# The loop over two layers written out: one copy of the program per layer on each engine

## The reference

```python
def first_block(x, positions, ...):
    cos, sin = rope_tables(positions)
    h = x
    for l in range(DEPTH):          # DEPTH = 2, D_MODEL = 1024, D_FF = 2816
        h = layer_norm(DEEPNORM_ALPHA * h + 0.5 * swiglu(h, ffn1_w_gate[l], ffn1_w_up[l], ffn1_w_down[l]),
                       ln1_g[l], ln1_b[l])
        mix = hybrid_mixer(h, cos, sin, w_in[l], b_gate[l], ...)   # delta rule, convolution, attention
        h = layer_norm(DEEPNORM_ALPHA * h + mix, ln2_g[l], ln2_b[l])
        h = layer_norm(DEEPNORM_ALPHA * h + 0.5 * swiglu(h, ffn2_w_gate[l], ffn2_w_up[l], ffn2_w_down[l]),
                       ln3_g[l], ln3_b[l])
    return h

def swiglu(x, w_gate, w_up, w_down):
    return (jax.nn.silu(x @ w_gate) * (x @ w_up)) @ w_down
```

## Time and profile before

| what | value |
|---|---|
| time, median of 3 runs | 3097.96 us (3096.59 to 3101.69) |
| the profiled execution, its span | 3106.6 us |
| PE busy in it | 2952.7 us, 95% |
| DVE, ACT, POOL busy | 2016.3, 1454.0, 50.5 us |
| TensorE's mean granted clock | 0.968 of full speed |
| the first block's two layers | 0 to about 1628 us |

### The profile page before, as it was taken

How to read it: one execution, slowest core, us unless ns; L and a number is a source line. 1 busy time by engine, 2 the same in 40 slices (tenths; PEclk the granted TensorE clock), 3 DMA queues, 4 the chain that set the end, 5 groups by cost and what they waited for, 6 DMA issues and landing times.

```text
span 3106.6 us, 44687 instructions
## 1 busy us (share of the span) xinstructions
PE 2952.7 (95%) x16782; PEld 2488.4 (80%) x16782; DVE 2016.3 (65%) x2457; ACT 1454.0 (47%) x1612; POOL 50.5 (2%) x93
## 2 busy tenths in 40 slices
PE   7999898999899998899999999998999999999997
PEld 7998886599899988766997599554888888888886
DVE  6767862377677679325770355143887888888987
ACT  5443521144344453213431154233777667766765
POOL 2000010000000000000000000000000000000000
PEclk9999989999899999989999999998999999999999
DMA  8754412287576543117763365323999999999995
GB/s 288 243 168 162 156 55 70 95 271 237 181 266 229 184 134 106 46 59 239 244 216 108 123 194 171 116 101 108 329 341 329 352 333 342 327 350 339 337 331 215
DMA packets 396807, 659.84 MB, mean 212 GB/s; under 512 B 12010, under 2 KB 239192, under 8 KB 396696
## 3 DMA queue, kind: packets, MB, share of 16 engines
q1 hardware_dynamic: 396696, 658.32, 61.5%
HBM read 657.23 MB, written 1.05 MB: 212 GB/s over the span
## 4 chain that ended last, share of the span: by engine, by line
PE 71%; DVE 9%; PEld 6%; issue 5%; ACT 4%; DVEq 2%; DMA 1%; PEldq 1%; ACTq 1%; SPq 0%
PE banks L711 18%; PE banks L712 17%; PE banks L713 17%; PE banks L2085 3%; PE banks L2117 3%; PE banks L1389 2%; PE banks L707 1%; PE banks L879 1%; PE banks L784 1%; PEld banks L1225 1%; DVE expert_rest L1113 1%; DVE ffn_arena L1052 1%; DVE mod_sum L1045 1%; PEld banks L711 1%; PE banks L885 1%
## 5 line engine op out<-in xcount | busy, mean ns | idle before, releaser
L711 PE MATMUL banks<-ffn_arena 128*128 128x256 f32 (+1 forms) x3460 | 1164.6, 337 | 43.2 <-DVE ffn_arena L1073 17.2
L713 PE MATMUL banks<-ffn_arena 128*128 128x256 f32 (+1 forms) x3460 | 1149.7, 332 | 0.0
L711 PEld LDWEIGHTS banks<-ffn_arena 128*128 128x128 f32 x3460 | 661.6, 191 | 117.7 <-issue 39.1
L713 PEld LDWEIGHTS banks<-ffn_arena 128*128 128x128 f32 x3460 | 661.0, 191 | 68.8
L1113 DVE TENSOR_TENSOR expert_rest<-expert_raw,ffn_arena 128x2048 fp32r<-128x2048 f32 (+1 forms) x306 | 646.1, 2159 | 85.8 <-ACT ffn_arena L972 81.4
L712 PE MATMUL banks<-ffn_arena 128*128 128x256 f32 (+1 forms) x2200 | 672.9, 306 | 0.0
L972 ACT ACTIVATE ffn_arena<-expert_raw 128x2048 fp32r<-128x2048 f32 (+1 forms) x306 | 538.9, 1816 | 110.4 <-PE banks L713 107.2
L712 PE MATMUL banks<-expert_rest,ffn_arena 128*128 128x512 f32 (+1 forms) x1224 | 466.6, 381 | 0.0
L712 PEld LDWEIGHTS banks<-ffn_arena 128*128 128x128 f32 x2200 | 423.9, 193 | 17.4 <-issue 0.5
L1052 DVE TENSOR_TENSOR ffn_arena<-gate_w,ffn_arena 128x1024 fp32r<-128x1024 f32 x110 | 129.9, 1222 | 215.2 <-ACT ffn_arena L908 215.2
L712 PEld LDWEIGHTS banks<-expert_rest,ffn_arena 128*128 128x128 f32 x1224 | 230.1, 188 | 42.5
(11 more groups left out here) (415 smaller groups left out, 3573.9 us busy)
## 6 DMA issues: line engine op xcount, KB each, us to landing
expert_raw<-in_moe_w_gate_dram SPq DMA_DIRECT2D x90, 1024.0 KB, 5.2
expert_raw<-in_moe_w_up_dram SPq DMA_DIRECT2D x90, 1024.0 KB, 5.6
expert_raw<-in_moe_w_down_dram SPq DMA_DIRECT2D x90, 1024.0 KB, 5.0
gate_w<-in_ffn_w_gate_dram SPq DMA_DIRECT2D x55, 1024.0 KB, 5.4
up_w<-in_ffn_w_up_dram SPq DMA_DIRECT2D x55, 1024.0 KB, 5.4
down_w<-in_ffn_w_down_dram SPq DMA_DIRECT2D x55, 1024.0 KB, 5.5
mod_unit<-in_mod_w_dram SPq DMA_DIRECT2D x48, 1024.0 KB, 5.2
panel<-in_w_in_dram SPq DMA_DIRECT2D x44, 1024.0 KB, 5.4
```

The costliest lines, as they stand in the source:

```text
L711: mm(out, w[0], x[0], start=start, stop=False)
L713: return mm(out, w[1], x[0], start=False, stop=stop)
```

## The change

On every engine the loop over the layers becomes a Python loop, which writes the layer's instructions out twice, with l = 0 and l = 1 as plain numbers. The functions that are called stay the same. Wait values and addresses that depended on l alone become constants; the loop inside each FFN stays, with its register s.

```diff
@@ -564,7 +564,7 @@
-            with sp.Fori(0, DEPTH) as l:
+            for l in range(DEPTH):
                 n = l * FFN_LAYER
                 mod = a["mod_w_2"][bass.ds(l, 1)]
...
@@ -677,7 +677,7 @@
-            with pool.Fori(0, DEPTH) as l:
+            for l in range(DEPTH):
...
@@ -2037,7 +2037,7 @@
-            with pe.Fori(0, DEPTH) as l:
+            for l in range(DEPTH):
                 n = l * FFN_LAYER
                 turn_h(pe, l * 6)
                 ffn_pe(pe, n, l * 2)
...
@@ -2212,7 +2212,7 @@
-            with act.Fori(0, DEPTH) as l:
+            for l in range(DEPTH):
                 n = l * FFN_LAYER
                 gate_act(act, n, 0)
                 turned_act(act, l * 12)
...
@@ -2342,7 +2342,7 @@
-            with dve.Fori(0, DEPTH) as l:
+            for l in range(DEPTH):
                 n = l * FFN_LAYER
                 gate_vec(dve, n, 0)
                 turned_vec(dve, l * 2)
```

## The result

The changed kernel takes **3078.59 us** (median of 4 runs, 3070.06 to 3082.54); the kernel before takes 3098.82 in the runs beside it (median of 4, 3096.59 to 3101.69). The ratio is 0.993, with a 95% interval of 0.9914 to 0.9946. The direction was right and the size half of the truth.

What follows compares the result with a forecast made beforehand. TensorE, busy 95% of the span, was taken as the bound, so only its pauses could shrink: 4.1 (junction) + 1.0 (start) + 4.6 (registers) + 0.3 (FFN ends) = 10.0 us, giving 3088.0 us; range 3080 to 3096.

Steps and rivals of the forecast that it cites:

- The junction: Change from layer one to two: ACT's taken branch (2.85 us) and its table load (1.29) go, 4.1 us gained.
- ACT's stall: At the change of layers, 2.73 us without activity behind ACT's loop branch, on the serial chain ACT, DVE, PE.
- PE's branch: At the change of layers, 3522 ns long but hidden under L885's matmuls, so counted at 0.
- the turns of H: PE's work due next at the change of layers, ending at 827.43; some 0.5 us of cover left, so 4.1 stands.
- The 9 us that come from counting every engine's stall: Branch stalls of PE, DVE and ACT added, 3.52 + 2.8 + 2.73; the prediction rejected this for 2.73 on the chain.
- The table load: In front of ACT's L908, executed in both layers; goes with the branch, 1.29 us at the change of layers.
- The start: Kernel's beginning: no table load and an earlier first transfer, 0.8 to 1.6 us until DVE's first mod_unit, taken as 1.0.
- Register operations and the FFNs' ends: Register instructions for waits and addresses, mostly in the mixers, 4.6 us; ends of four FFNs, 0.3 us.
- PE's part: Some 40 register operations of PE on the first block's chain, 0.09 us each: 3.6 us, taken whole.
- Rival (3): Looped code no longer fits and is refetched, perhaps at ACT's expert loop ends: 12 us slower, 3110; chance 0.04.
- What the inner loop costs with registers: FFN passes take 16.97 us with n in a register or constant, so the first block's 40 passes give 0.
- The term of the clock: TensorE's drops to its lower clock taken as unrelated to code: 0 in the sum, some 3 us in the range.

Runs made afterwards that it cites:

- e3: Kernel before with the layer loop written out on PE, DVE, POOL and SP, ACT keeping its loop: 3084.0 us.
- e2: Kernel before with only ACT's layer loop written out: 3096.9 us.
- e5: Kernel before with only PE's layer loop written out: 3095.5 us.
- e7: Kernel before with only SP's and POOL's layer loops written out: 3099.7 us.
- e6: Kernel before with only DVE's layer loop written out: 3096.6 us.
- e16: Kernel before with DVE's, SP's and POOL's layer loops written out, PE and ACT keeping theirs: 3094.3 us.
- e13: Changed kernel with eight drains on PE in each layer, ahead of the turns before the attention scores: 3089.2 us.
- e14: e13 with three matmuls nobody reads added in PE's pause behind the turns, before the scores: 3075.5 us.
- e11: Kernel before, loops kept, with three matmuls nobody reads in PE's pause before the attention scores: 3097.1 us.
- e15: Kernel before with PE's and DVE's layer loops written out, the others kept: 3086.6 us.
- e1: Kernel before, unchanged, run again as a control: 3099.8 us.
- e4: Changed kernel with two loops of one pass, one per layer, on every engine instead of straight code: 3078.9 us.
- e8: Changed kernel, run again unchanged: 3076.6 us.
- e12: Changed kernel with three matmuls nobody reads in PE's pause before the attention scores: 3075.2 us.

## Why the prediction was wrong in size and right in its sum

**The sum was right in total.** It gave 10.0 us; at an equal clock the change is worth 10.8 (error 1), and by parts:

- The junction: 4.1 predicted; from L707 to L711 4.5 measured in the trace (10.52 to 6.02). That in the kernel before ACT's stall counts, and not PE's 3.5 or DVE's, stands: e3 keeps ACT's alone and has 2.38 us of it in its chain. But PE's branch isn't worth nothing once ACT's is gone: in e2 0.80 us of it are exposed, and the junction gains 3.4 us there. The prediction asked what is late next for DVE and for the turns of H, not for PE's branch ahead of them. The 9 us that come from counting every engine's stall, by the rule of the Trainium skill ("Runtime: NRT & Kernel Launch", "Instruction fetch mechanics"), aren't borne out as time: the stalls are there, two of them under other work. The table load took 1.28 us in every trace. The Trainium skill ("ScalarE: Activation LUTs", "What ACT_TABLE_LOAD costs") adds a drain of about 1380 ns to it; this case's trace has none: in the kernel before, the load at L1578 starts 0.02 us behind the end of the activation before it, and the next activation 0.01 us behind the load.
- The start: 1.0 predicted, 1.36 in the trace.
- Register operations and the FFNs' ends: 4.9 predicted; 10.8 less 4.5 and 1.4 leaves 4.9. That the two agree so well is in part luck, as too much on PE and too little on DVE cancel. PE's part was 3.6 and measured 2.8 (e5); SP's was put at 0.8, of which the sum took a third, and e7 has 0.7 with the start's earlier issue in it. That DVE's would be small was wrong: 3.7 by e6, though e16, in which DVE is joined by SP and POOL, shows only 1.9; their errors overlap at the edges, and DVE's share is probably between them.
- Rival (3), code that is fetched again in loops: no. 73 and 31 packets, and the branches that stay are as short as they were.
- What the inner loop costs with registers: nothing, as said; the pass is the same in all profiles.

**The step that failed** is "TensorE's clock falls to its lower level (1.2 of 2.4 GHz) for short stretches at points that don't belong to the code, so any shift of the work may win or lose some 3 us; no part of the sum rests on it, but the range does". The term of the clock was put at 0 with 3 us of blur, and measured about 10: 20 us of gain, less the 10.8 at an equal clock. The first half of the sentence was only a part of the truth. At the scores, whether the level falls depends on a pause of PE (e13 against e14), and where the program stands relative to such a moment repeats from run to run. So a shift wasn't noise of 3 us with a mean of zero: in the profiles both layers lost the same fall, 4.7 us each, 9.4 in all. It was there to be read: the page's row of the clock, and behind it the two stretches of 24 us at 0.72 in the kernel before, at the same lines in both layers. I had looked at the clock of the two mixers, seen that they differed by 0.02, and concluded that it was chance; I hadn't looked at what they had in common.

**What stays open.** Why the distance from the code to those moments is alike in nearly all runs at the scores, though the runs begin at any distance to them. Why e11 gained 2.5 us and not 10. Whether in e13 the later arrival or the longer standstill ahead of the turns brings the fall. Which register operations of PE and DVE, between where and where, make up the few tenths; e15, e5 and e6 say that the two together bring more than each alone, and nothing finer. Not all of the clock's gain is at the scores: by span and mean clock the profiles of before, e1, e2, e6 and e7 have some 184 us at the lower level (span x 2 x (1 less the clock)), those of the changed kernel, e3, e4 and e8 some 134. The two falls at the scores are 27 of these 50 us. The rest is at other places of the first block, some of it between 450 and 540 us, not as regularly, and no run tests them.

## What to carry to other kernels

A taken branch on an engine and the table load at a loop's head cost what the chain of waits shows of them, not what their rows last; when one stall is taken away, ask also which of the others it had covered. And in a kernel that TensorE bounds, ask of each longer matmul stretch at the lower clock whether it stands behind the same pause in each repetition: if so, it may be a cost of that pause, which here a few tenths of a us switched on or off. Matmuls of no use in the pause took the falls away in each profile that has them; they gave time back in e14 and next to none in e11 and e12, so measure the whole kernel. Compare kernels at an equal mean clock, which each run states, before explaining a difference by instructions.

## What the runs showed of the hardware that I had not expected

- A delay of 0.63 us per layer, ahead of the turns and the pause of 1.05 us behind them, cost 11 us in all (e13), and 1.3 us of matmuls without use in that pause gave 13.7 back (e14).
- The mean clock of one unchanged kernel ranges from 0.967 to 0.976 over 87 runs, 23 us in time (3090.7 to 3113.9), with one slope of 2.3 us for 0.001.
- A layer's code written out twice on all engines was fetched in fewer blocks (104 packets) than the loop (111). It goes with the way back to a loop's head: 2 packets fewer with PE's loop gone (e5), 3 with ACT's (e2), 3 with DVE's (e6), none with SP's and POOL's (e7), and in e4, which has loop heads and no way back, 103.
